# A bidirectional HGRN2 scan on one core: where the gates' affine step and the factor 1 - lb are applied

## The reference

```python
def _forget_gates(z, lb):
    zf = z.astype(jnp.float32)
    f = lb + (1.0 - lb) * jax.nn.sigmoid(zf)
    log_f = jnp.log(jnp.maximum(f, F_FLOOR))
    k = (1.0 - lb) * jax.nn.sigmoid(-zf)
    return _heads(k), _heads(log_f)

def _chunk_scan(q, k, v, log_f, s0):
    ...
        o_inter = jnp.einsum("bhtk,bhkv->bhtv", qc * jnp.exp(cum), s)
        ...
        scores = jnp.einsum("bhtk,bhsk,bhtsk->bhts", qc, kc, decay)
        o = o_inter + jnp.einsum("bhts,bhsv->bhtv", scores, vc)
        ...
        s_new = jnp.exp(last[:, :, 0, :])[..., None] * s + jnp.einsum(
            "bhsk,bhsv->bhkv", kc * jnp.exp(last - cum), vc)
```

## Time and profile before

| what | value |
|---|---|
| median of 3 runs | 3011.87 us (3010.69 to 3012.3) |
| profiled execution, its own time | 3009.45 us |
| profiled execution, span first to last instruction | 3007.4 us |
| TensorE busy | 2823.2 us, 94% |
| VectorE busy | 1437.7 us, 48% |
| ScalarE busy | 731.5 us, 24% |
| GpSimd busy | 762.7 us, 25% |
| mean granted TensorE clock | 0.975 |

### The profile page before, as it was taken

The page is one execution under the profiler, slowest core; times in us unless marked ns, Lnnn a source line. Parts: engine busy times, 40 slices in busy tenths (PEclk is TensorE's granted clock), DMA queues, the critical chain, the costliest instruction groups (busy, mean ns, idle before and its releaser), DMA issues.

```text
span 3007.4 us, 36416 instructions
## 1 busy us (share of the span) xinstructions
PE 2823.2 (94%) x13776; PEld 2367.2 (79%) x13776; DVE 1437.7 (48%) x2063; ACT 731.5 (24%) x1271; POOL 762.7 (25%) x361
## 2 busy tenths in 40 slices
PE   6989889999996799999999998999899999999997
PEld 4778778778875688888888886888778888888886
DVE  5276676576569232343332346555832322332235
ACT  4323223223223242111111115211143111111112
POOL 3212112121215311222222232344612222222222
PEclk9999999999997799999999999999999999999999
DMA  5110111111110201121211110333200111111111
GB/s 225 57 42 29 64 36 38 55 36 56 36 36 28 98 15 47 46 77 49 77 63 63 61 57 30 108 119 110 91 15 29 49 50 49 49 49 49 49 49 70
DMA packets 48742, 176.89 MB, mean 59 GB/s; under 512 B 5872, under 2 KB 5872, under 8 KB 48624
## 3 DMA queue, kind: packets, MB, share of 16 engines
q1 hardware_dynamic: 48624, 175.24, 16.9%
HBM read 171.02 MB, written 4.19 MB: 58 GB/s over the span
## 4 chain that ended last, share of the span: by engine, by line
PE 80%; DVE 12%; ACT 4%; issue 3%; DMA 1%; POOL 1%; DVEq 0%; SPq 0%; ACTq 0%; POOLq 0%
PE psum L594 17%; PE psum L596 17%; PE psum L595 17%; PE psum L989 4%; PE psum L990 4%; PE psum L991 4%; PE psum L773 3%; DVE q_all L1644 2%; DVE k_all L1637 2%; PE psum L823 2%; PE psum L824 2%; PE psum L825 2%; PE psum L637 1%; DVE h_lo L1471 1%; PE psum L787 1%
## 5 line engine op out<-in xcount | busy, mean ns | idle before, releaser
L594 PE MATMUL psum<-h_hi,w_hi 128*128 128x512 f32 x2336 | 939.1, 402 | 11.5 <-POOL w_lo L506 4.8
L596 PE MATMUL psum<-h_hi,w_lo 128*128 128x512 f32 x2336 | 914.2, 391 | 0.0
L595 PE MATMUL psum<-h_lo,w_hi 128*128 128x512 f32 x2336 | 913.7, 391 | 0.0
L549 POOL TENSOR_TENSOR w_lo<-w_raw,w_hi 128x1024 fp32r<-128x1024 f32 x116 | 280.0, 2413 | 1031.1 <-ACT w_hi L1099 1031.1
L594 PEld LDWEIGHTS psum<-h_hi,w_hi 128*128 128x128 f32 x2336 | 441.9, 189 | 95.0 <-POOL w_lo L506 5.2
L596 PEld LDWEIGHTS psum<-h_hi,w_lo 128*128 128x128 f32 x2336 | 440.7, 189 | 94.5
L595 PEld LDWEIGHTS psum<-h_lo,w_hi 128*128 128x128 f32 x2336 | 442.1, 189 | 81.2
L503 POOL TENSOR_TENSOR w_hi<-w_raw,zero 128x1024 fp32r<-128x1024 f32 x74 | 152.0, 2054 | 1058.9 <-PE psum L594 946.5
L1471 DVE TENSOR_TENSOR hidden<-gate_act,up_copy 128x512 f32<-128x512 f32 x88 | 75.8, 861 | 654.8 <-ACT up_copy L1099 654.8
L1471 DVE TENSOR_TENSOR y<-y,psum 128x512 f32<-128x512 f32 x288 | 195.0, 686 | 202.3 <-PE psum L991 199.8
L989 PE MATMUL psum<-w_hi,hidden_hi 128*128 128x512 f32 x640 | 250.2, 391 | 0.3 <-DVE y L1471 0.3
(11 more groups left out here) (213 smaller groups left out, 3558.2 us busy)
## 6 DMA issues: line engine op xcount, KB each, us to landing
w_raw<-in_w_ffn_in SPq DMA_DIRECT2D x88, 512.0 KB, 3.5
ada_raw<-in_ada SPq DMA_DIRECT2D x80, 512.0 KB, 4.3
w_raw<-in_w_ffn_out SPq DMA_DIRECT2D x44, 512.0 KB, 3.5
w_raw<-in_w_hgrn_in SPq DMA_DIRECT2D x40, 512.0 KB, 6.2
w_raw<-in_w_conv_in SPq DMA_DIRECT2D x24, 512.0 KB, 4.6
ada_first<-in_ada SPq DMA_DIRECT2D x4, 2048.0 KB, 15.1
x_start<-in_x SPq DMA_DIRECT2D x4, 1024.0 KB, 19.0
w_raw<-in_w_hgrn_out SPq DMA_DIRECT2D x8, 512.0 KB, 3.7
```

The source lines that it names most:

```text
L549: pool.tensor_tensor(lo[:, :], w_raw[:, slot, :], hi[:, :], ALU.subtract).then_inc(S["panel_split"], 1)
L594: begin = pe.matmul(out_ap, hi[:, a:b], rhs_hi, start=first, stop=False)
L595: pe.matmul(out_ap, hi[:, a:b], rhs_lo, start=False, stop=False)
L596: return begin, pe.matmul(out_ap, lo[:, a:b], rhs_hi, start=False, stop=last)
```

## The change

ScalarE does the affine step of the gates: after the four sigmoids two more activations (Identity, scale 1 - lb, bias lb, both read from memory, one column of a tile each). VectorE keeps the maximum alone. The keys are no longer multiplied by 1 - lb; instead the queries are, by their evacuation's scale, which is now read from the tile `head_scale`. VectorE fills this tile once per head from `q_scale` = (1 - lb) times 128 ** -0.5, which it makes once at the start. `constants` takes the number it waits for.

```diff
@@ constants and the scan's start on ScalarE
+                    floor, room = lb[:, bass.ds(hs, 1)], one_minus_lb[:, bass.ds(hs, 1)]
                     for d in (FWD, BWD):
                         copy(gates[d][:, :], z[d][:, :], "sigmoids", ACT.Sigmoid)
                         copy(k[d][:, :], z[d][:, :], "sigmoids", ACT.Sigmoid, scale=-1.0)
+                    act.wait_ge(S["sigmoids"], hs * 4 + 3)
+                    constants(1)
+                    for d in (FWD, BWD):
+                        copy(gates[d][:, :], gates[d][:, :], "gates_scaled", ACT.Identity, scale=room, bias=floor)
                     for part in range(3):
...
-                        act.wait_ge(S["gates_done"], hs * 6 + 7)
+                        act.wait_ge(S["gates_done"], hs * 2 + 3)
...
-                    evacuate(2, 0, cols(q, 0), scale=float(P) ** -0.5)
+                    act.wait_ge(S["head_scaled"], hg + 1)
+                    evacuate(2, 0, cols(q, 0), scale=head_scale[:, 0:1])
...
-                    evacuate(2, 1, cols(q, 1), scale=float(P) ** -0.5)
+                    evacuate(2, 1, cols(q, 1), scale=head_scale[:, 0:1])
@@ VectorE
+            V.tensor_scalar(q_scale[:, :], one_minus_lb[:, :], float(P) ** -0.5, None, ALU.mult
+                            ).then_inc(S["params"], 1)
...
+                def scale_of_head():
+
+                    V.tensor_copy(head_scale[:, :], q_scale[:, bass.ds(hg, 1)]).then_inc(S["head_scaled"], 1)
...
                     for d in (FWD, BWD):
-                        dve.wait_ge(S["sigmoids"], hs * 4 + (2 * d + 1))
-                        V.tensor_scalar(gates[d][:, :], gates[d][:, :], oml, lbs, ALU.mult, ALU.add
-                                        ).then_inc(S["gates_done"], 1)
-                        dve.wait_ge(S["sigmoids"], hs * 4 + (2 * d + 2))
-                        V.tensor_scalar(k[d][:, :], k[d][:, :], oml, None, ALU.mult).then_inc(S["gates_done"], 1)
-                        dve.wait_ge(S["gates_done"], base_g + (3 * d + 1))
+                        dve.wait_ge(S["gates_scaled"], hs * 2 + (d + 1))
                         V.tensor_scalar(gates[d][:, :], gates[d][:, :], F_FLOOR, None, ALU.max
                                         ).then_inc(S["gates_done"], 1)
-                    dve.wait_ge(S["gates_done"], base_g + 6)
+                    dve.wait_ge(S["sigmoids"], hs * 4 + 4)
+                    if hg is not None:
+                        scale_of_head()
+                    dve.wait_ge(S["gates_done"], hs * 2 + 3)
                     tt(k_sum[:, :], lat(k[FWD]), lat(k[BWD]), ALU.add, "diag_ready")
```

More of the change, by code:

```diff
@@ L241, in build_trunk @@
     one_minus_lb = small("one_minus_lb", KB)
+    q_scale = small("q_scale", KB)
+    head_scale = small("head_scale", 1)
     gn = small("gn", 1)
@@ L272, in build_trunk @@
             sigmoids gates_done diag_ready scan_f scan_b k_merged scan_full scan_evac scores_evac state_f state_b
-            gate_sig gs_ready o_squared o_gated o_sum_full ovar_done orstd_ready mix_ready mods_ready
+            gates_scaled gate_sig head_scaled gs_ready o_squared o_gated o_sum_full ovar_done orstd_ready mix_ready mods_ready
             mix_hi mix_split
@@ L1099, in copy, with constants @@
                 nc.scalar.activation(dst, src, func, **kw).then_inc(S[sem], 1)
-            def constants():
-                act.wait_ge(S["consts"], 5)
+            def constants(n=5):
+                act.wait_ge(S["consts"], n)
             def x_norm(inst, block, junk):
@@ L1235, in head @@
                     act.wait_ge(S["gemm_evac"], hs * 10 + (4 + O_HEADS + 10))
-                    constants()
+                    constants(2)
                     copy(mix[:, bass.ds(hs, 1), :], g[:, :].unsqueeze(1), "gate_sig", ACT.Sigmoid)
@@ L1678, in head @@
                 if hs is not None:
-                    lbs, oml = lb[:, bass.ds(hs, 1)], one_minus_lb[:, bass.ds(hs, 1)]
-                    base_g = hs * 6 + 1
                     for d in (FWD, BWD):
-                        dve.wait_ge(S["sigmoids"], hs * 4 + (2 * d + 1))
-                        V.tensor_scalar(gates[d][:, :], gates[d][:, :], oml, lbs, ALU.mult, ALU.add
-                                        ).then_inc(S["gates_done"], 1)
-                        dve.wait_ge(S["sigmoids"], hs * 4 + (2 * d + 2))
-                        V.tensor_scalar(k[d][:, :], k[d][:, :], oml, None, ALU.mult).then_inc(S["gates_done"], 1)
-                        dve.wait_ge(S["gates_done"], base_g + (3 * d + 1))
+                        dve.wait_ge(S["gates_scaled"], hs * 2 + (d + 1))
                         V.tensor_scalar(gates[d][:, :], gates[d][:, :], F_FLOOR, None, ALU.max
                                         ).then_inc(S["gates_done"], 1)
-                    dve.wait_ge(S["gates_done"], base_g + 6)
+                    dve.wait_ge(S["sigmoids"], hs * 4 + 4)
+                    if hg is not None:
+                        scale_of_head()
+                    dve.wait_ge(S["gates_done"], hs * 2 + 3)
                     tt(k_sum[:, :], lat(k[FWD]), lat(k[BWD]), ALU.add, "diag_ready")
```

## The result

| | before | changed |
|---|---|---|
| median | 3009.43 us (3006.48 to 3012.3, 6 runs) | 3025.29 us (3018.86 to 3030.81, 6 runs) |
| profiled execution, its own time | 3009.45 us | 3021.3 us |
| span | 3007.4 us | 3019.3 us |
| VectorE busy | 1437.7 us | 1397.2 us |
| ScalarE busy | 731.5 us | 752.9 us |

The ratio is 1.0055, with a 95% interval of 1.0042 to 1.0068: 16.5 us slower, 12.6 to 20.5 (the medians alone are 15.9 us apart). VectorE works 40 us less and nobody is helped. The profiled pair is 11.85 us apart; it is one execution of each.

A forecast was written before the change was run, and what follows sets the result against it. TensorE, busy 94% of the span, was taken as the bound. Terms 9.85 + 1.28 + 2.69 = 13.8 us on 3009.45 gave 3023.3, and with the runs' median 2.4 higher 3025.7 us; range 3016 to 3034.

The forecast's parts named there:

- The slack of 0.55 us at the third transpose: Scan at 473.39: TensorE's third transpose starts 5.84 us after the first sigmoid and could start at 5.29.
- A pass: ScalarE's added Identity before v_tok: 1.17 + 0.175 us, two 2.69; lower end 2.33, upper end 4.08 a pass.
- The five scans: Scan at 473.39 and four alike: new third-transpose wait 2.14 us, 0.17 absorbed before the diagonal, net 1.97 x 5 = 9.85 us.
- The two scans behind the loop's jump: Scans beginning a loop pass, third transpose already at 7.30 and 7.38 us: net 0.68 + 0.60 = 1.28 us.
- The last scan: ScalarE is on the path to level 0 there, so everything moves by the two passes, 2.69 us.
- The gain on VectorE: Four operations and a 2 us collision fewer per scan, worth nothing; k_sum at 8.5 us against 8.29, covered.
- A fall of the clock later in a scan: TensorE's granted clock dropping to half after level 0, in six of seven scans: 2.26 us each.
- The queries' evacuation: 16 evacuations of q with scale from memory: at most 0.175 us longer each, 2.8 us upper end, taken as nothing.
- the balance of the clock: Net effect of TensorE clock falls gained and lost: taken as zero, between -19.5 and +7.4 us.
- a fall behind each new wait: Rival: half clock after the new waits in five scans, 5 x 1.48 = 7.4 us, total 21.2 us; chance 0.19.
- the loss of the four falls after level 0: Rival: half-clock spells after level 0's wait go, 13.8 - 5.9 = 7.9 us slower; chance 0.18.
- Faster: Rival: passes at their lower end and all ten clock falls gone, 10.9 - 19.5 = -8.6 us; chance 0.03.

The follow-up runs named there:

- e2: Changed kernel with only the affine step on ScalarE; VectorE multiplies the keys and q has its constant again: 3031.01 us, ratio 1.0066 to the kernel before.
- e1: Changed kernel with only the queries' factor; affine step back on VectorE, keys unscaled, no added ScalarE passes: 3008.3 us, ratio 0.9995 to the kernel before.
- e3: Changed kernel with the first v_tok evacuation ahead of ScalarE's two passes: 3009.52 us, ratio 1.0 to the kernel before.
- e4: Changed kernel with the two passes as plain copies, no scale or bias, so no affine step: 3016.72 us, ratio 1.0019 to the kernel before.
- e7: Kernel before with level 0's k_both copies ahead of the evacuation of z_f's second half on ScalarE: 2995.77 us, ratio 0.9953.
- e8: e1 with the edit of e7 (queries' factor alone, level 0's copies first): 2989.65 us, ratio 0.9937 to the kernel before.
- e9: Changed kernel, the whole change, with level 0's k_both copies first as in e7: 3011.29 us, ratio 1.001 to the kernel before.
- e6: As e3, with k_sum ahead of the gates' maxima on VectorE: 3009.95 us, ratio 0.9999 to the kernel before.
- e5: Changed kernel with two more ScalarE passes, in-place copies of the gates, ahead of v_tok: 3052.36 us, ratio 1.0138 to the kernel before.

## Why the prediction was right

**The place and the mechanism were right.** The slack of 0.55 us at the third transpose, read from the last scan, held: where the third transpose waits for it, the release comes 0.63 us after `v_tok` begins, at 7.98 us as worked out, to the hundredth. e2 and e1 put the loss into the affine half, and e3 into the order of ScalarE: one evacuation in front of the passes instead of behind them.

**The terms of the sum.**
- A pass: 1.35 us predicted (2.69 the pair), 1.34 measured (484.18 to 485.53 to 486.87). The choice against the upper end, by which the pointers cost by the element, was right: Identity took 1.440 us where a sigmoid takes 1.257, and the plain copy of the same size in e4 takes 1.257 too. e4 has the lower end: `v_tok` at 6.98.
- The five scans: 1.97 us net each predicted. Without the fall of 1.59, first sigmoid to level 0 grew by 1.84 to 1.95 us.
- The two scans behind the loop's jump: 0.68 and 0.60 predicted. One grew by 0.73. The other grew by 1.55 and did not wait for `v_tok` at all, since a fall of the clock (0.50 from 593.9 to 597.0), ahead of the transposes, had held TensorE up. Its third transpose comes 8.93 us after the first sigmoid, without a wait:

```profile
601.54 0.38 PE L747 MATMUL psum<-ident,v_t 128*128 128x128 f32 x2
```

- The last scan: 2.69 predicted, 2.41 at its level 0 (18.04 against 15.63 us after the first sigmoid). But not all of that reaches the end. From the last scan's first sigmoid to the product behind the scaled projection it takes 127.04 us before (906.90 to 1033.94), 125.36 with the change (922.56 to 1047.92) and 129.86 in e2 (927.77 to 1057.63), which has the same two passes. So in the changed kernel's profile this term is -1.7 us and not +2.69, and what falls of the clock and other waits do in this stretch is larger than the term.
- VectorE: `k_sum` at 8.5 us predicted (8.4 to 8.6 in the signs), 8.34 measured, with no one waiting for it in the five scans. The gain on VectorE was worth nothing that the times can tell, as e1 shows by itself.
- A fall of the clock later in a scan: 2.26 us predicted, from two scans of different heads. With the same heads it is 1.6 us. In e7, level 0 to the next first sigmoid takes 91.71 us where no fall lies between them (scans at 146.27 and 359.07) and 93.28 where one does (251.93). The head at 815.85 is some 0.6 us shorter by itself (91.1 without a fall). So the ten falls hold about 15.5 us and not 19.5.
- The queries' evacuation: 0.688 us with the factor from memory against 0.598, at no cost on the path (e1).

**The term that was mis-sized most is the balance of the clock**, put at zero. I had a fall behind each new wait (5 x 1.48) as a rival with a chance of 0.19, and the loss of the four falls after level 0 as another with 0.18. In the profiled execution both happened together, five new ones of 1.59 us and none after level 0 where there were four: +7.9 and -5.9 us. The later falls moved about as well, seven by the trace against six, two scans with two of them and two with none, and one new fall came at the start of the scan at 592.61. Thirteen falls against ten, at 1.58 us each, are 4.7 us. Taken off the 16.3 us by which the seven scans grew, they leave 11.6 us, where the sum has 9.85 + 1.28 = 11.1: without the clock the forecast of these scans was right to half a microsecond. So zero was too low for the clock by 4.7 us in this execution and the last scan's 2.69 was too high, and the two errors partly cancel; my list had the new falls and the lost ones as alternatives, where both came.

The 16.5 us measured stand against 13.8 predicted by the sum, and 3025.3 against 3025.7 us. That the two times agree so closely is partly luck, for the kernel before turned out at 3009.4 in six runs where three had given 3011.9, and the change is 2.7 us larger than the sum.

**The rivals.** "Faster" needed all the falls to go; e7 and e8 come near to that, with three and two falls instead of ten, but by another edit. That Identity would need another table did not happen.

**What stays open.** Why a fall comes behind a wait in one scan and not in the next. In front of the third transpose, waits of 1.94 to 2.01 us had a fall behind them in 5 of 5 scans in the changed kernel and in e2, but in 3 of 5 in e9, and waits of 1.56 to 1.62 us in 0 of 5 in e4. In front of level 0, waits of 1.4 to 1.6 us had one in 4 of 7 scans in the kernel before, e1 and e6, in 2 in e2, in 1 in e5, and in none in the changed kernel, e3 and e4. So the length of the wait alone does not decide it, and the runs here do not separate what does.

## What to carry to other kernels

A pass that is moved to an idle engine stands in that engine's list in front of something: look up what is queued behind it, and how many hundred nanoseconds that has before the bounding engine asks for it. Here 40 us less work on VectorE were worth nothing and 2.7 us a scan in front of a 0.6 us evacuation cost 16 us; with that evacuation first the same work costs nothing that can be measured (e3, e6). An operation saved pays where its engine is the last one in. The saved key products brought level 0 forward by 0.25 us in e1 and by 0.68 once level 0's copies had been moved ahead of an evacuation (e8 against e7), and that move, worth 14 us, did most by itself.

## What the runs showed of the hardware that was not expected

- **A wait of TensorE can cost 1.6 us more than its length.** In e9 the same wait of 1.96 us cost 2.0 us in one scan and 3.6 in another, by whether a fall of the clock followed. In e4 the waits are 0.37 us shorter and none of the five falls came; the kernel was 10.8 us less slow by the ratios, where the waits and the last scan's shift alone account for 2.9 by the sum.
- **Falls come and go with small shifts of everything before them.** In e3, where the diagonal is 0.55 us later, none of the four falls behind level 0's wait of 1.51 us came, and that hid the cost of the shift. In e6, which has no such shift, they are back.
- **A pointer operand costs ScalarE a fixed 0.09 us.** 1.440 against 1.257 us for two pointers at 1280 columns (the changed kernel against e4's plain copies), 0.688 against 0.598 for one at 512. The Trainium skill gives the same figure, about 93 ns ("ScalarE: Activation LUTs", section "What ACT_TABLE_LOAD costs"), and the traces agree.
- **VectorE's operation that met GpSimd's split took 2.90 us instead of 0.94**, in e1 too. In the changed kernel VectorE's first operation comes after `w_lo` has ended (480.76 + 2.41 = 483.17 against 485.65), and takes 0.83 us. The kernel before has one pattern in all eight scans: VectorE's operation ends 0.68 or 0.69 us after the end of the GpSimd instruction under which it begins (474.62 + 2.42 = 477.04 against 474.82 + 2.90 = 477.72), whether it has 2.4 us of that instruction still before it or 0.3. It takes 2.9 to 3.1 us in five scans, 1.0 and 1.3 in the two behind the loop's jump and 1.8 in the last. No run has it without GpSimd's instruction and otherwise the same, so the cause is read from the rows alone. This time went off VectorE's list, and none of it lay on the path.
